# Output projection by token tile, branch tiles among its steps, and cache copies in two stages

## Time and profile before

| | us |
|---|---|
| median of 3 runs (1133.82, 1133.91, 1136.89) | 1133.91 |
| the profiled execution | 1137.22 |
| its span in the trace | 1135.4 |
| TensorE busy | 1055.9 |
| VectorE, ScalarE, GpSimd busy | 565.8, 392.6, 232.6 |
| granted TensorE clock, mean | 0.973 |

### The profile page before, as it was taken

One profiled execution on the slowest core, in us unless ns is written; L12 is line 12 of the kernel. 1 busy time (PEld: TensorE's weight loads), 2 busy tenths in 40 slices (PEclk: granted clock), 3 DMA queues, 4 the chain that ended last, 5 costly groups with the idle time before them and its releaser, 6 DMA issues.

```text
span 1135.4 us, 19822 instructions
## 1 busy us (share of the span) xinstructions
PE 1055.9 (93%) x7458; PEld 913.1 (80%) x7458; DVE 565.8 (50%) x928; ACT 392.6 (35%) x838; POOL 232.6 (20%) x429
## 2 busy tenths in 40 slices
PE   5999999999999699999978993999999999999994
PEld 4777877677777699989968772999999999877773
DVE  4452242533245678876314329467666666522214
ACT  5233233233233233323213255344544444312312
POOL 2101020312201454542512303200000000011003
PEclk9999999999999899999999895999999999999997
DMA  5633343334443677765773630434434434342222
GB/s 211 222 121 130 112 143 128 137 129 170 146 165 115 200 236 241 223 226 164 258 261 130 236 130 0 144 133 153 148 119 166 148 133 144 123 152 100 97 96 81
DMA packets 40765, 175.17 MB, mean 154 GB/s; under 512 B 7242, under 2 KB 7690, under 8 KB 39168
## 3 DMA queue, kind: packets, MB, share of 16 engines
q1 hardware_dynamic: 25472, 125.66, 31.1%
q0 software_dynamic: 15232, 48.65, 13.6%
HBM read 164.28 MB, written 54.05 MB: 192 GB/s over the span
## 4 chain that ended last, share of the span: by engine, by line
PE 83%; DMA 4%; DVE 4%; ACT 3%; issue 2%; POOL 2%; SPq 0%; DVEq 0%; ACTq 0%; POOLq 0%
PE bank L1177 12%; PE bank L1179 11%; PE bank L1178 11%; PE bank L1258 11%; PE bank L1252 11%; PE bank L1257 11%; PE bank L1196 3%; PE bank L1410 2%; DMA qbc<-sample_queries 2%; PE bank L1388 2%; PE bank L1159 2%; DMA kvv<-in_cache_kv_g 2%; PE bank L1348 1%; PE bank L1342 1%; ACT whi L753 1%
## 5 line engine op out<-in xcount | busy, mean ns | idle before, releaser
L1595 DVE TENSOR_TENSOR wlo<-wraw,whi 128x1024 fp32r<-128x1024 f32 x96 | 118.6, 1237 | 367.1 <-ACT whi L753 367.1
L1252 PE MATMUL bank<-T1h,whi 128*128 128x272 f32 x960 | 280.8, 292 | 0.2 <-issue 0.2
L1258 PE MATMUL bank<-T1h,wlo 128*128 128x272 f32 x960 | 279.3, 291 | 0.0
L1257 PE MATMUL bank<-T1l,whi 128*128 128x272 f32 x960 | 277.5, 289 | 0.0
L753 ACT ACTIVATE whi<-wraw 128x1024 fp32r<-128x1024 f32 x98 | 103.7, 1058 | 370.9 <-PE bank L1179 286.8
L1252 PEld LDWEIGHTS bank<-T1h,whi 128*128 128x128 f32 x960 | 182.5, 190 | 2.8 <-issue 2.6
L1257 PEld LDWEIGHTS bank<-T1l,whi 128*128 128x128 f32 x960 | 182.5, 190 | 0.2
L1258 PEld LDWEIGHTS bank<-T1h,wlo 128*128 128x128 f32 x960 | 181.9, 190 | 0.0
L1177 PE MATMUL bank<-whi,T1h 128*128 128x512 f32 (+1 forms) x352 | 140.7, 400 | 1.6 <-DVE etmp L1734 1.6
L1178 PE MATMUL bank<-wlo,T1h 128*128 128x512 f32 (+1 forms) x352 | 136.0, 386 | 0.0
L1179 PE MATMUL bank<-whi,T1l 128*128 128x512 f32 (+1 forms) x352 | 135.9, 386 | 0.0
(11 more groups left out here) (268 smaller groups left out, 1740.0 us busy)
## 6 DMA issues: line engine op xcount, KB each, us to landing
wraw<-in_weights SPq DMA_DIRECT2D x142, 512.0 KB, 3.5
out_s_kv_g<-in_cache_kv_g SPq DMA_DIRECT2D x64, 511.0 KB
qbc<-sample_queries POOLq DMA_DIRECT2D x48, 256.0 KB, 4.8
kvk<-in_cache_kv_g POOLq DMA_DIRECT2D x32, 256.0 KB, 3.7
kvv<-in_cache_kv_g POOLq DMA_DIRECT2D x16, 512.0 KB, 9.3
out_s_kv_g<-in_cache_kv_g SPq DMA_DIRECT2D x16, 508.0 KB
S<-in_state_ret POOLq DMA_DIRECT2D x16, 256.0 KB, 7.4
out_s_ret<-S POOLq DMA_DIRECT2D x16, 256.0 KB, 2.6
```

Source lines behind the costliest of these rows:

```text
L1252: one = mm(dst, Wh, Th[:, k, c], start=k == 0, stop=False)
L1257: mm(dst, Wh, Tl[:, k, c], start=False, stop=False)
L1258: last = mm(dst, Wl, Th[:, k, c], start=False, stop=k == kt - 1)
L1595: v.tensor_tensor(wlo[:, s % 2, :], wraw[:, s % 2, :], whi[:, s % 2, :].bitcast(F), ALU.subtract).then_inc(w_lo, 1)
```

## The change

- **Output projection.** The first block stays slot by slot (`out_step`). In the second block all four slots are held in split form at once, and TensorE goes tile by tile (`out_rows`): tile 0, 1, 2, 3. The sample rows of the second block go into bank 5 (`second_sample`), two slots during the first block's last step and two at tile 0. The halves of slots 68 to 71 and of 72, 74 and 75 lie in buffers of their own (`w_halves`), so their splits wait for other things than before.
- **Norms.** Order: sample rows first, then tiles 0 to 3 (`NORM_ORDER`). The residual add moves from GpSimd to VectorE (in `mixed`). The transposes of the sample rows, tiles 0 and 1 are issued inside the second block's tiles 2 and 3; those of tiles 2 and 3 between the first up matmuls.
- **Up projection.** The columns of its input are reordered to tile 0, tile 1, sample rows, tile 2, tile 3, and its halves are 288 and 256 wide. The first halves of slots 76 and 77 are done first, then the second ones.
- **Branch tiles.** They use banks 5 to 7 in turn; six come first, then output step 0, the last two, and steps 1 to 3. The add of the retention branch moves from GpSimd to VectorE.
- **Raw buffers.** `w_seen` is raised ahead for slots 42 to 67 (`ahead`) and for the 44 up slots at once.
- **Cache copies.** 44 in slots 2 to 41, the other 44 in slots 78 to 117, 11 per 10 slots; none between.
- **GpSimd.** `conv_state` is loaded when slot 75 is used up; only two columns of each part of `ub` are cleared.

```diff
+NORM_ORDER = (4, 0, 1, 2, 3)
+ROOTS = {key: n + 1 for n, key in enumerate((("m", 0), ("m", 1), ("h", 0), ("h", 1), ("m", 2), ("h", 2), ("m", 3), ("h", 3), ("m", 4), ("h", 4)))}
+HEAD_COLS = {0: slice(0, 128), 1: slice(128, 256), 4: slice(256, 288), 2: slice(288, 416), 3: slice(416, 544)}
+UP_HALVES = ((0, 288), (288, 256))
...
+    order += [(("ba", n, half), 5 + (2 * n + half) % 3) for n in range(KT) for half in range(2)]
+    order.append((("os",), 5))
+    for p, i in enumerate(NORM_ORDER):
         for half in range(2):
-            order.append((("h2", i, half), 5 + (2 * i + half) % 3))
+            order.append((("h2", i, half), 5 + (2 * p + half) % 3))
...
+    def w_halves(s):
+        if S_OUT <= s < S_OUT + 4:
+            return out_split[s - S_OUT][:, 0, :], out_split[s - S_OUT][:, 1, :]
+        if s in apart_hi:
+            return apart_hi[s][:], apart_lo[s][:]
+        return whi[:, s % 2, :], wlo[:, s % 2, :]
...
-        with sp.Fori(0, NB) as b:
-            for e in range(8):
-                load(b * 16 + (2 + 2 * e))
-                move(2, b, e, 8)
-                if e % 4 == 1:
-                    move(1, b, e // 4, 2)
-                if e == 3:
-                    move(0, b, 0, 1)
-        with sp.Fori(0, (NSLOT - 130) // 2) as it:
-            load(it * 2 + 130)
+        def load_beside_moves(first, b0):
+            with sp.Fori(0, NB // 2) as it:
+                for e in range(5):
+                    load(it * 10 + (first + 2 * e))
+                    for piece in ((0, 1), (2, 3), (4, 5), (6,), (7,))[e]:
+                        move(2, it + b0, piece, 8)
+                    if e == 3:
+                        move(1, it + b0, 0, 2)
+                    if e == 4:
+                        move(1, it + b0, 1, 2)
+                        move(0, it + b0, 0, 1)
+        load_beside_moves(2, 0)
+        with sp.Fori(0, (S_UP + 2 - 42) // 2) as it:
+            load(it * 2 + 42)
+        load_beside_moves(S_UP + 2, NB // 2)
+        with sp.Fori(0, (NSLOT - S_UP - 42) // 2) as it:
+            load(it * 2 + (S_UP + 42))
...
-        for n in range(KT):
-            pool.wait_ge(a_free[n % 2], 13 + n // 2)
-            nc.gpsimd.tensor_tensor(mtmp[:, n % 3, :], mtmp[:, n % 3, :], mixr[:, n, :], ALU.add).then_inc(mix_sum, 1)
...
-        for i in range(TILES):
-            r = rows(i)
-            pool.wait_ge(x_again[i], 16)
-            pool.wait_ge(x_scaled, i + 1)
-            nc.gpsimd.tensor_tensor(xo[0:r, i, :], tmpn[0:r, i % 2, :], xr[0:r, i, :], ALU.add).then_inc(x2_ready, 1)
-        filled(pool, ("h2", 4, 1))
-        emptied(pool, ("h2", 4, 1))
+        pool.wait_ge(w_used, S_UP)
         pool.dma_start(cvs[:], a["conv_state"]).then_inc(cvs_in, 16)
-        step(nc.gpsimd.memset(ub[:], 0.0))
+        filled(pool, ("h2", NORM_ORDER[-1], 1))
+        pool.wait_ge(n_rt, 2 * TILES)
+        step(nc.gpsimd.memset(ub[:, :, :, 0:2], 0.0))
...
+            if S_OUT <= s <= S_OUT + 4:
+                act.wait_ge(w_used, S_BA)
+            elif s in (S_OUT + 5, S_UP):
+                act.wait_ge(w_used, S_BA + (1 if s == S_UP else 2))
+            elif s in (S_OUT + 6, S_OUT + 7):
+                act.wait_ge(mix_sum, KT)
+            elif s >= 2:
                 act.wait_ge(w_used, s - 1)
-            nc.scalar.activation(whi[:, s % 2, :], wraw[:, s % 2, :], ACT.Copy).then_inc(w_hi, 1)
+            nc.scalar.activation(w_halves(s)[0], wraw[:, s % 2, :], ACT.Copy).then_inc(w_hi, 1)
...
+        w_split(S_OUT + 4)
+        tile_end(BLK_OUT, 4)
+        sample_rows(P[4], 512, xo[0:TS, 4, 0:512], ((512, 1.0),)).then_inc(b_free[4], 1)
+        w_split(S_OUT + 5)
+        out_evac(0)
+        out_evac(1)
+        w_split(S_OUT + 6)
+        out_evac(2)
+        out_evac(3)
+        half_square(4)
+        act.wait_ge(half_sq, 1)
+        half_square(0)
+        w_split(S_OUT + 7)
+        for i in (1, 2, 3):
+            act.wait_ge(half_sq, i + 1)
+            half_square(i)
+        act.wait_ge(half_sq, TILES)
+        step(nc.scalar.activation(njunk[:, 0:1], eps[:, 0:1], ACT.Sqrt))
+        w_split(S_UP)
...
+        mixed_root(0)
+        mixed_root(1)
+        hidden_root(0)
+        hidden_root(1)
+        mixed_root(2)
+        hidden_hi(0)
+        hidden_root(2)
+        hidden_hi(1)
+        mixed_root(3)
+        hidden_hi(2)
+        hidden_root(3)
+        mixed_root(4)
+        w_split(S_UP + 1)
+        hidden_hi(3)
+        hidden_root(4)
+        hidden_hi(4)
...
+                        ones[0].then_inc(w_seen, len(pair) + (ahead if s + 2 >= n else 0))
...
+        b_block(BLK_RG + 1, *T1, between=lambda s: turn_gated(0) if s == 2 else None, ahead=S_OUT - S_GB)
...
+        def out_step(s):
+            pe.wait_ge(mix_lo, 2 * s + 2)
+            last = out_sample(BLK_OUT, s, P[4])
+            last.then_inc(b_full if s == 3 else w_seen, 1)
+            if s == 3:
+                second_sample(0)
+            pe.wait_ge(w_lo, S_OUT + s + 1)
+            for i in range(4):
+                if s == 3 and i == 3:
+                    second_sample(1)
+                last = out_tile(BLK_OUT, i, s, seen=1 if s == 3 and i == 0 else 0)
+                if s == 3:
+                    if i < 3:
+                        last.then_inc(b_full, 1)
+                    else:
+                        last.then_inc(w_used, 4)
...
+        for n in range(6):
+            branch(n)
+            if n == 4:
+                branch_slot_done(3)
+        pe.wait_ge(a_free[0], 12)
+        pe.wait_ge(a_free[1], 12)
+        for i in range(5):
+            pe.wait_ge(b_free[i], BLK_OUT)
+        out_step(0)
+        branch(6)
+        branch(7)
+        out_step(1)
+        branch_slot_done(7)
+        out_step(2)
+        out_step(3)
...
+        def out_rows(p, turned):
+            i = NORM_ORDER[p]
+            pe.wait_ge(b_free[i], BLK_OUT + 1)
+            for s in range(4):
+                if p == 1:
+                    pe.wait_ge(w_lo, S_OUT + 4 + s + 1)
+                if p == 1 and s < 2:
+                    second_sample(2 + s)
+                if s in turned:
+                    turn_hidden(turned[s])
+                last = out_tile(BLK_OUT + 1, i, s, full=p == 1 and s == 0, seen=1 + S_DN - S_UP if p == 1 and s == 1 else 0)
+            if i == 3:
+                last.then_inc(w_used, 4)
+            else:
+                last.then_inc(b_full, 1)
+        out_rows(1, {})
+        out_rows(2, {})
+        out_rows(3, {1: 0, 3: 1})
+        out_rows(4, {2: 2})
...
+        head_ready_for(2)
+        head_ready_for(1)
+        pe.wait_ge(b_free[0], BLK_OUT + 2)
+        pe.wait_ge(b_free[2], BLK_OUT + 2)
+        pe.wait_ge(w_lo, S_UP + 1)
+        pe.wait_ge(u_evac[0], 1)
+        pe.wait_ge(u_evac[1], 1)
+        up_half(0, 0)
+        turn_hidden(TILES - 2)
+        pe.wait_ge(w_lo, S_UP + 2)
+        up_half(1, 0)
+        turn_hidden(TILES - 1)
+        pe.wait_ge(b_free[1], BLK_OUT + 2)
+        pe.wait_ge(b_free[3], BLK_OUT + 2)
+        pe.wait_ge(b_free[4], BLK_OUT + 2)
+        head_ready_for(TILES - 2)
+        head_ready_for(TILES - 1)
+        up_half(0, 1).then_inc(w_used, 1)
+        up_half(1, 1).then_inc(w_used, 1)
...
+        def branch_gated(n):
             if n >= 3:
                 dve.wait_ge(mix_lo, n - 2)
-            gated(n, sga[:, n, :], 2 * p, mtmp[:, n % 3, :], a_free[p])
-            if n == 4:
-                w_split(S_OUT)
+            for half in range(2):
+                key = ("ba", n, half)
+                b = filled(dve, key)
+                c = slice(HALF * half, HALF * half + HALF)
+                v.scalar_tensor_tensor(mtmp[:, n % 3, c], sga[:, n, c], 1.0, b[:, 0:HALF], ALU.add, ALU.mult
+                                       ).then_inc(bank_free[USES[key][0]], 1)
+            emptied(dve, ("ba", n, 0))
+            emptied(dve, ("ba", n, 1))
+            v.tensor_tensor(mtmp[:, n % 3, :], mtmp[:, n % 3, :], mixr[:, n, :], ALU.add).then_inc(mix_sum, 1)
+        for n in range(KT):
+            branch_gated(n)
+            if n in (1, 3, 5, 7):
+                w_split(S_OUT + n // 2)
...
+        def mixed(p):
+            i = NORM_ORDER[p]
             r = rows(i)
+            dve.wait_ge(n_rt, ROOTS["m", p])
+            scaled(tmpn[:, p % 2, :], xo, i, 0, gpost, x_scaled)
+            dve.wait_ge(x_again[i], 16)
+            dve.wait_ge(x_scaled, p + 1)
+            v.tensor_tensor(xo[0:r, i, :], tmpn[0:r, p % 2, :], xr[0:r, i, :], ALU.add).then_inc(x2_ready, 1)
...
+        mixed(0)
+        mixed(1)
+        hidden(0)
+        hidden(1)
+        mixed(2)
+        hidden_lo(0)
+        hidden(2)
+        hidden_lo(1)
+        mixed(3)
+        hidden_lo(2)
+        hidden(3)
+        mixed(4)
         w_split(S_UP + 1)
+        hidden_lo(3)
+        hidden(4)
         hidden_lo(4)
```

(45 more changed lines are left out.)

230 lines of the change are left out of this document (113 added, 117 removed).

## The result

The changed kernel takes 1118.7 us (median of 4 runs, 1118.29 to 1119.11) where the kernel before took 1135.0 in the same comparison: ratio 0.985 [0.983, 0.987]. The forecast was 1114 us, range 1104 to 1125, and faster: 19.6 us less, where 16.3 and 19.2 were measured.

What follows compares the result with a forecast made beforehand. TensorE was busy 93%, so only its idle and low-clock time could be won. Tail -14.4, attention start -2.7 and sample values -2.5 sum to -19.6 us, from a median of 1133.9 to 1114 us, range 1104 to 1125.

Steps and rivals of the forecast that it cites:

- Attention start, -2.7: Start of the attention: without cache copies among key and query reads, the fourth query piece lands sooner, 2.7 us won.
- Sample values, -2.5: Sample values beside gate tiles: two waits for `kvv` totalling 5.6 us shrink, mainly by removing a copy, 2.5 us won.
- the prediction's own doubt: Sample values: longest `kvv` wait has no copy near it, said against both DMA waits going nearly whole (1106 us, chance 0.17).
- Tail, -14.4: Branch stage to up stage: up starts 16.6 us earlier in full-clock terms, less charges of 1.5 and 0.7: 14.4 us won.
- GpSimd's 687 to 690 DMAs: Output projection, after the first half's steps: the reload, issued at about 642, has 20 us of cover.
- The charges: Tail: 1.5 us for one clock drop behind TensorE's waits and 0.7 us for waiting on slot 78's split.
- hn at 1.27, not 3.46: Second norm: VectorE's `hn` product takes 1.27 us once GpSimd has no add there, instead of 3.46.
- Add at 1.23: Second norm: the residual add of 1024 elements, new on VectorE, takes 1.23 us, priced by a split of the same shape.
- Branch tiles between output steps: Branch stage: the first output step can start at 623.9 us against 629.18, with branches 6 and 7 run behind it.
- Copies elsewhere 0: Slots 2 to 41 and up stage: denser cache copies stay hidden behind the weight loads, 0 us (bounds 0 and +7).
- raw buffers 0: Loads of slots 44 to 69 and the up stage start about one slot sooner, where TensorE never waits: 0 us.
- the 4 us that the prediction took from this rule: Attention start: if DMA engines alternate between queues, the copies' 1.0 MB cost 4 us; the prediction kept 2.7 from landings.

Runs made afterwards that it cites:

- copies_alone: The kernel before with only the new cache copy loop (44 beside slots 2 to 41, 44 beside 78 to 117), raw buffers freed as before: ratio 0.998 to before.
- copies_undone: The changed kernel with the cache copies issued the old way, beside slots 2 to 129: ratio 0.986 to the kernel before.
- loads_later: The changed kernel, but GpSimd reloads x and the two gains only once slot 73's raw weights have landed: ratio 0.983 to the kernel before.
- adds_on_gpsimd: The changed kernel with the second norm's five residual adds back on GpSimd, the order of the rest kept: ratio 0.989 to the kernel before.
- branches_first: The changed kernel with all eight branch tiles before the first output step, splits of slots 70 and 71 moved later: ratio 0.983 to the kernel before.
- reload_early: The changed kernel with the sample rows' and tiles 0 and 1's transposes one insertion later and the x and gains reload spread over the branch stage: ratio 0.982 to before.
- no_adds: The changed kernel with the second norm's five residual adds left out, x still reloaded: ratio 0.981 to the kernel before.

## Why the prediction was right, step by step

The forecast of the sum is within 0.4% and the order of its terms is right. Of its three sizes one is right, one is too large, and one is right by errors that cancel, so part of the closeness is luck.

*Attention start, -2.7: right.* The matmul behind the score wait starts at 391.4 and 392.1 in the two profiles with the old code in front of it, at 387.2 to 391.3 (mean 389.1) in ten with the change's: 2.7 us. The wait itself fell by as much (6.8 to 4.1). But the copies and the early freed buffers each suffice, and the prediction gave the second 0.

*Sample values, -2.5: too much, and its cause not shown.* From there to the branch start: 217.9 and 218.5 before, mean 216.5 of the ten (214.3 to 218.2): 1.7 us, in ranges that overlap. The first profile's 3.0 was a good draw. With the copies moved alone nothing is gained here (218.3). `kvv` is waited for 4.7 us after and 6.5 before, 5.1 in copies_alone, but 4.5 in copies_undone with copies in this stretch. So the runs do not show copies as the price here; the prediction's own doubt, that the longest wait has no copy near it, fits.

*Tail, -14.4: right in the sum (13.9 and 14.3), by two errors.* Shifted by the 4.5 us that the branch starts sooner, my times against the profile: output step 0 at 619.4 (619.0); end of the first half 650.5 (655.1); root of the sample rows through at 661.9 (664.7); last low half 695.3 (697.0); up's remaining half 695.4 (697.2). The branch stage is right. The step that failed, inside a term whose sum came out, is "GpSimd's 687 to 690 DMAs are issued at about 642, with 20 us of cover": I gave the reload cover for its own landing and did not ask whose landing it stretches. It cost 4.4 us of waiting and the clock of 650 to 656 (0.53). In the kernel before, the reload was issued 23.7 us behind the branch start, just behind two weight loads that landed in 3.4 and 4.4 us; putting two branch tiles behind step 0 moved it to 31.8. VectorE's chain took back part: from root to last low half it took 32.3 us for my 33.4. The charges took back the rest: the clock was at 1.00 where the up stage starts, and the stage's 262.9 us are 0.9 over what it took before at full clock (978.5 - 708.6 - 6.4 - 1.5 = 262.0), for 2.2 charged. TensorE's waits were 2.7, 0, 1.1 and 1.7 for 3.8, 1.4, 2.0 and 1.7.

*hn at 1.27, not 3.46: right*, five products at 1.27 to 1.29. *Add at 1.23: right* (1.21 to 1.23).

*Branch tiles between output steps.* I gave this part no price of its own. It brings 1.2 us in the stage and, by the reload that it moves, costs more at slot 73: without it the stretch is 3.2 us shorter.

*Copies elsewhere 0, raw buffers 0:* right for the up stage; copies left in the output projection would cost 2.3 to 2.7.

Open: how the 14 us divide between rows first and tiles in place of steps. The profile shows that the waits for `hn` are gone, and the runs price the adds (about 6), but the rest, the larger part, is argued from the order and no kernel isolates it. The last 0.9 us of the up stage were not looked into. Why a load waits behind the reload before its first packet (below) is open too.

## What to carry to other kernels

A transfer with cover enough for itself can still be the reason why a short load is late. So for each burst list the loads with little slack that are issued behind it in its 8 to 12 us, and ask again whenever an edit moves the burst. Filling TensorE's pauses is worth what it still idles there after the other edits, which may be little. When a serial chain over three engines sets a start, keep the hand overs few: the same add took 1.2 us on VectorE, the chain's own engine, and 2.3 and more on GpSimd, before any hand over.

## What the runs showed of the hardware

A weight load of 512 KB landed in 3.5 us alone. Issued behind the first transfers of the reload (seven transfers, 3.3 MB) it took 7.5 to 8.5 us in ten of the profiles. The packets by queue show where the 4.9 us of slot 73's load (issued 642.3) went. From 642.3 to 646.3 only the reload's queue q0 moved packets, and from 646.3 to 650.7 both did (packets, MB, share of the 16 engines, which comes out a little over 100; q1 is SyncE's queue, with the loads of slots 73 and 74):

```profile
q0 software_dynamic: 392, 1.38, 102.2%
```
```profile
q1 hardware_dynamic: 235, 0.89, 52.6%
q0 software_dynamic: 211, 0.76, 47.1%
```

Alone, a load's first packet comes 1.0 us behind its issue; here it came after 4.1, and after 3.8 for slot 75's in `loads_later`. So 3.1 of the 4.9 us passed before the first packet, and only the rest is sharing. The Trainium skill ("DMA: Bandwidth & Descriptors", Queues, rings and completion order) has the engines alternate between queues with work. From the first packet on the trace agrees: 53% to 47%. For the 3.1 us by which that packet came late it does not, and no run shows why they pass. At the attention's start the 4 us that the prediction took from this rule were too much (2.7).

In the kernel before, VectorE's products were stretched beside GpSimd's adds, and the adds were not: an add took 2.34 us beside a product and 2.37 with none beside it in `adds_on_gpsimd` (at 675.2). By the profile the product had even started 0.04 us ahead of its add (694.81 and 694.85, and the earlier trace rows).

TensorE's clock behind pauses: 0.72 from 650 to 660 behind the wait of 4.4 us, 0.79 from 672 to 680 behind the one of 2.7. In `branches_first` and `reload_early` the waits for weights of 1.4 and 2.0 us were followed by 1.00. A wait's length alone does not decide: behind 1.7 us before up's remaining half the clock was 1.00 in the changed kernel and 0.57 in `no_adds`.
